# Moving the q, k and attention-gate projections into one stage with the SSD scans

## The reference, cut to what matters

```python
h = rms_norm(x, norm_in);  proj = h @ w_in          # 1024 -> q k v z_attn z_ssd xbc dt_f dt_b
xbc = silu(depthwise_conv(xbc))                     # x (16 heads x 64), B, C (2 groups x 128)
y_ssd = rms_norm((ssd_scan(x, dt_f, B, C) + flip(ssd_scan(flip(...dt_b...))) + d_skip * x) * silu(z_ssd))
#   per chunk of 128 tokens: lmat = exp(acum_l - acum_s) for s <= l;  y_diag = (C B^T * lmat) @ (x * dt)
#   states are carried from chunk to chunk;  y_off = (C @ state) * exp(acum)
y_attn = dilated_mixture(rotary(q), rotary(k), v) * silu(z_attn)   # windows 128/1, 512/4, 2048/16
out = rms_norm(x + concat(y_ssd, y_attn) @ w_out)
```

## Time and profile before

| | us |
|---|---|
| median of 3 runs | 4325.24 (4322.37 to 4328.68) |
| the profiled execution | 4329.58 |
| its span | 4328.0 |
| granted TensorE clock, mean | 0.940 |
| PE busy, DVE busy, ACT busy, POOL busy | 3837.7, 2332.8, 1266.6, 1890.2 |

### The profile page before, as it was taken

How to read it: one execution, slowest core, us unless ns; L and a number is a source line. 1 busy time by engine, 2 the same in 40 slices (tenths; PEclk the granted TensorE clock), 3 DMA queues, 4 the chain that set the end, 5 groups by cost and what they waited for, 6 DMA issues and landing times. The chain is left out here.

```text
span 4328.0 us, 59482 instructions
## 1 busy us (share of the span) xinstructions
PE 3837.7 (89%) x21061; PEld 2920.7 (67%) x21061; DVE 2332.8 (54%) x4451; ACT 1266.6 (29%) x3501; POOL 1890.2 (44%) x1451
## 2 busy tenths in 40 slices
PE   6999999999899998876777777688989999699999
PEld 5887778887788887752333333566666777588887
DVE  4401534403524205416888888577777888556564
ACT  2011220011220012210222222566666777322222
POOL 5444253534344444406999999332233233200000
PEclk9999999999999999988888888899999999799999
DMA  4333242322243232317222222544444344444442
GB/s 160 98 97 94 70 138 88 104 93 79 73 142 102 92 105 65 95 53 288 72 88 89 92 90 76 130 114 107 111 109 116 105 127 118 149 166 152 157 153 108
DMA packets 332015, 483.38 MB, mean 112 GB/s; under 512 B 27772, under 2 KB 228548, under 8 KB 329732
## 3 DMA queue, kind: packets, MB, share of 16 engines
q1 hardware_dynamic: 300867, 365.58, 26.5%
q0 software_dynamic: 26304, 94.78, 7.5%
q10 hardware_dynamic: 4608, 19.92, 1.4%
HBM read 315.04 MB, written 165.15 MB: 111 GB/s over the span
## 5 line engine op out<-in xcount | busy, mean ns | idle before, releaser
L253 POOL TENSOR_TENSOR front_w_hi<-front_w_raw,one 128x1024 fp32r<-128x1024 f32 (+1 forms) x168 | 303.0, 1803 | 929.9 <-PE front_out L475 918.4
L1488 ACT ACTIVATE attn_p_sb<-attn_p_sb,attn_o_sb 128x256 f32<-128x256 f32 (+1 forms) x1152 | 534.9, 466 | 305.1 <-DVE attn_o_sb L1522 300.7
L1522 DVE CUSTOM_DVE_ANT_0 attn_p_sb<-attn_s_ps,attn_mask 128x256 f32<-128x256 f32 (+1 forms) x1152 | 368.7, 376 | 166.1 <-DMA s_o<-attn_o_sb 125.9
L406 DVE TENSOR_SCALAR front_acc<-front_chan,front_consts 128x1024 f32<-128x1024 f32 (+2 forms) x36 | 38.9, 1080 | 714.3 <-ACT front_chan L296 714.3
L1315 POOL COPY attn_q_apart<-attn_q 128x128 f32<-128x128 f32 (+2 forms) x256 | 136.7, 534 | 645.5 <-PE attn_s_ps L1421 639.6
L256 POOL TENSOR_TENSOR front_w_lo<-front_w_raw,front_w_hi 128x1024 fp32r<-128x1024 f32 (+1 forms) x168 | 411.4, 2449 | 13.2
L475 PE MATMUL front_out<-front_h_hi,front_w_hi 128*128 128x512 f32 x1392 | 358.6, 401 | 8.9 <-DVE front_turned L386 3.6
L475 PE MATMUL front_out<-front_h_hi,front_w_lo 128*128 128x512 f32 x1392 | 346.3, 391 | 0.0
L475 PE MATMUL front_out<-front_h_lo,front_w_hi 128*128 128x512 f32 x1392 | 344.0, 389 | 0.0
L960 PE MATMUL ssd_seg<-ssd_spread,masks 128*128 128x512 f32 x384 | 250.3, 793 | 95.4 <-POOL ssd_spread L899 95.4
L475 PE MATMUL front_out<-front_w_hi,front_h_hi 128*128 128x512 f32 x1152 | 291.2, 394 | 29.0 <-POOL front_w_lo L256 29.0
(11 more groups left out here) (178 smaller groups left out, 6882.1 us busy)
## 6 DMA issues: line engine op xcount, KB each, us to landing
front_w_raw<-w_in POOLq DMA_DIRECT2D x156, 512.0 KB, 4.3
s_o<-attn_o_sb SPq DMA_DIRECT2D x288, 132.0 KB, 2.1
output_parts<-s_o SPq DMA_DIRECT2D x24, 1584.0 KB, 6.6
back_xb<-s_xb ACTq DMA_DIRECT2D x24, 640.0 KB, 6.2
ssd_xb<-s_xb SPq DMA_DIRECT2D x24, 640.0 KB, 4.0
s_q<-front_stage SPq DMA_DIRECT2D x48, 256.0 KB, 2.2
s_k<-front_stage SPq DMA_DIRECT2D x48, 256.0 KB, 2.2
s_zs<-front_stage SPq DMA_DIRECT2D x48, 256.0 KB, 3.5
```

The source lines that it names most:

```text
L253: nc.gpsimd.tensor_tensor(hi, raw, one.to_broadcast([P, 2, cols]), ALU.mult).then_inc(sem["w_hi_ready"], 1)
L406: nc.vector.tensor_scalar(a, chan[:, 0:conv.tokens], consts[:, conv.ct:conv.ct + 1], consts[:, TAPS * CHAN_TILES + conv.ct:TAPS * CHAN_TIL ...
L1488: last = nc.scalar.activation(cut, cut, ACT.Exp, scale=-1.0, bias=o_sb[g // 2 % ring][:, g % 2, h, VW:OW], accum_out=o_sb[g // 2 % ring][: ...
L1522: last = nc.vector.tensor_tensor_reduce(out=p_sb[g % 4][:, h, 0:width], in0=s_ps[g % 2][h][:, 0:width], in1=mask[:, step.pattern.strip(ste ...
```

## The change

q, k and za leave front (six of its fourteen groups; 144 units in all). Before the next block's `h` overwrites them, SP stores `h_hi` and `h_lo` of the first two blocks in DRAM (`scratch["h"]`); the third block's stay in SBUF. The backward-states and SSD stages are gone as stages of their own. After stats (which gets two more results: ln dt and the sums, laid out in `wide`) a short stage, `decay_rows_phase`, turns the 48 tiles of `wide` in six rounds (PE eight transposes, ACT a 128x1024 copy, DVE a 128x1024 operation) and stores 1.57 MB and twice 0.39 MB.

Then `late_phase` runs 144 **slots**. In each slot every engine does first a piece of the scans and then its share of one projection unit (24 matmuls, as in front). Slots 0 to 23 hold one backward chunk each; slots 24 to 143 hold 24 forward chunks of five parts each (`CYCLE`). Blocks are taken in the order 2, 1, 0, with q, k, za in each (48 units); at the change of a block ACT loads h half by half (4.19 MB a half). Weights come in pieces of 128 columns, 72 of them, split by POOL. Units of q and k are rotated by DVE, those of za get a Silu on ACT. za is now stored by channel, not by token, so the output stage reads it with 512-byte rows and applies it after the turn.

The scan itself is computed otherwise. The segment sums come from two fp32r matmuls with 64 rows of contraction and 512 columns (`decays`) on rows from DRAM, for forward and backward decay in a bank each; ACT copies the one, DVE overlays the other where s > l by `copy_predicated` (`choose`), ACT takes one exponential over 128x2048, and DVE multiplies by C·B from PSUM (`whole_m`, two of 128x1024). POOL's spreading and the 128x2048 additions on DVE are gone. POOL has, per chunk, `scale_x`, `keep_state`, `skip_x` and the two additions of `add_rest`, 128x1024 each. DVE has four `choose`, two `state_part` (128x1024, PSUM), two `next_state` (128x512, PSUM), two halves of `whole_m`, `gated` (two of 128x1024, one of them from PSUM), `finish`, and four small ones in `skip_part`. PE has four `decays`, `products`, two `state_part`, two `add_state` and `diagonal`, all but `decays` as before.

The core of the diff:

```diff
-    groups = [("rope", "q", 0), ("rope", "q", 1), ("rope", "k", 0), ("rope", "k", 1), ("silu", "zs", 0),
-              ("silu", "zs", 1), ("silu", "za", 0), ("silu", "za", 1), ("chan", "xbc", 0), ("chan", "xbc", 1),
+    groups = [("silu", "zs", 0), ("silu", "zs", 1), ("chan", "xbc", 0), ("chan", "xbc", 1),
               ("chan", "xbc", 2), ("dt", "dt", 0), ("v", "v", 0), ("v", "v", 1)]
...
                 j = t % BT
+                if t >= BT:
+                    act.wait_ge(sem["h_stored"], 32 * (t // BT))
                 nc.scalar.copy(h_hi[:, :, j * P:(j + 1) * P], tr[:, :, :]).then_inc(sem["h_high"], 1)
...
+                if unit.name == "zs" and unit.part == 1 and unit.j == 0 and unit.b + 1 < BLOCKS:
+                    sp.wait_ge(sem["h_split"], (unit.b + 1) * BT)
+                    for i, h in enumerate((h_hi, h_lo)):
+                        sp.dma_start(scratch["h"][unit.b, i, :, :, :], h[:, :, :].bitcast(F32)).then_inc(sem["h_stored"], 16)
...
+    units, ropes = [], 0
+    for turn, b in enumerate((2, 1, 0)):
+        for name in ("q", "k", "za"):
+            for pair in range(D_ATTN // (2 * P)):
+                for half in range(BLOCK // CW):
+                    for ab in range(2):
+                        unit = LateUnit(len(units), turn, b, name, pair, half, ab)
...
+            nc.gpsimd.memset(m[:, :, :], 0.0).then_inc(sem["f_rows_set"], 1)
+            for step, first in enumerate((0, HEADS, 64, 64 + HEADS)):
+                pool.wait_ge(sem["f_rows_set"], step + 1)
+                nc.gpsimd.affine_select(out=m[:, :, :], in_=m[:, :, :], compare_op=ALU.not_equal, fill=1.0,
+                                        base=-first, pattern=[[-1, HEADS], [0, P]], channel_multiplier=1
+                                        ).then_inc(sem["f_rows_set"], 1)
...
+            def split(w):
+                if w >= weights:
+                    return
+                if w >= 3:
+                    pool.wait_ge(sem["l_out"], last_use[w - 3] + 1)
...
+            weigh(0)
+            for slot in range(len(units)):
+                if slot + 1 < first_forward:
+                    weigh(slot + 1)
+                n, part = part_of(slot)
+                if part == 0:
+                    scale_x(n)
+                    keep_state(n)
+                if slot % 4 == 0:
+                    split(slot // 2 + 2)
+                if part == 2:
+                    skip_x(n)
+                if slot % 4 == 3:
+                    split(slot // 4 * 2 + 3)
+                if part == 4:
+                    add_rest(n)
...
+            for slot, unit in enumerate(units):
+                if slot < first_forward:
+                    store_back(slot)
...
+                n, part = part_of(slot)
+                if part == 1 and n:
+                    store_y(n - 1)
+                    load_gate(n)
+                if part == 4 and n + 1 < NT:
+                    load_rows(n + 1)
+                    load_states(n + 1)
+                if part == 1 and 2 <= n + 1 < NT:
+                    load_x(n + 1)
...
+                if slot:
+                    store(units[slot - 1])
...
+            def multiply(unit):
+                u, s = unit.u, unit.weight % 3
+                if unit.n >= 2:
+                    name, count = units[unit.n - 2].taken_by
+                    pe.wait_ge(sem[name][u], count)
+                if unit.turn and unit.n == first_of_half[unit.turn, unit.half]:
+                    pe.wait_ge(sem["l_h_in"][unit.half], 32 * unit.turn)
...
+            def scan(slot):
+                if slot < first_forward:
+                    add_back(slot)
+                n, part = part_of(slot)
+                if part == 0:
+                    if n:
+                        diagonal(n - 1)
+                    decays(n, 0)
+                elif part == 1:
+                    decays(n, 1)
+                    products(n)
+                    state_part(n, 0)
+                elif part == 2:
+                    decays(n, 2)
+                    add_state(n, 0)
+                elif part == 3:
+                    decays(n, 3)
+                    add_state(n, 1)
+                    state_part(n, 1)
+            for slot, unit in enumerate(units):
+                scan(slot)
+                multiply(unit)
+            diagonal(NT - 1)
...
+            def load_h(turn, half):
+                act.wait_ge(sem["l_out"], last_of_half[turn - 1, half] + 1)
+                b = (2, 1, 0)[turn]
+                cut = slice(half * CW, (half + 1) * CW)
+                for i, h in enumerate((h_hi, h_lo)):
+                    act.dma_start(h[:, :, cut].bitcast(F32), scratch["h"][b, i, :, :, cut]).then_inc(sem["l_h_in"][half], 16)
...
+            def rotate(unit):
+                u = unit.u
+                dve.wait_ge(sem["l_out"], unit.n + 1)
+                if u == 0:
+                    if unit.ropes_before:
+                        dve.wait_ge(sem["l_staged"][1], units[unit.n - 1].n // 2 if not units[unit.n - 1].rope else unit.n // 2)
+                    for a in range(2):
+                        last = nc.vector.tensor_tensor(a_turned[:, a, :], out[0][:, :], table[:, a, half], ALU.mult)
+                    last.then_inc(sem["l_taken"][0], 1)
+                    return
+                for a in range(2):
+                    dve.wait_ge(sem["l_stored"][a], 16 * (unit.n // 2))
+                    last = nc.vector.tensor_tensor(stage[:, a, :], out[1][:, :], table[:, 1 - a, half], ALU.mult)
+                last.then_inc(sem["l_taken"][1], 1)
+                dve.wait_ge(sem["l_taken"][1], unit.ropes_before // 2 + 1)
+                for a, op in ((0, ALU.subtract), (1, ALU.add)):
+                    nc.vector.tensor_tensor(stage[:, a, :], a_turned[:, a, :], stage[:, a, :], op
+                                            ).then_inc(sem["l_staged"][a], 1)
...
+            def gated(n):
+                dve.wait_ge(sem["f_rest"], 2 * n + 2)
+                dve.wait_ge(sem["f_diag"], n + 1)
+                nc.vector.tensor_tensor(y[:, :], y[:, :], work[:, :], ALU.add).then_inc(sem["f_y_steps"], 1)
+                dve.wait_ge(sem["f_y_steps"], 2 * n + 1)
+                dve.wait_ge(sem["f_gate_in"], 16 * (n + 1))
+                nc.vector.tensor_tensor(gate[:, :], y[:, :], gate[:, :], ALU.mult).then_inc(sem["f_y_steps"], 1)
...
+            def scan(slot):
+                if slot < first_forward:
+                    back_step(slot)
+                n, part = part_of(slot)
+                if part == 0:
+                    if n:
+                        gated(n - 1)
...
+                    choose(n, 0)
+                elif part == 1:
+                    choose(n, 1)
+                    if n:
+                        finish(n - 1)
+                    skip_part(n)
+                    state_part(n, 0)
+                elif part == 2:
+                    choose(n, 2)
+                    next_state(n, 0)
+                elif part == 3:
+                    choose(n, 3)
+                    next_state(n, 1)
+                    state_part(n, 1)
+                elif part == 4:
+                    whole_m(n)
...
+            for slot, unit in enumerate(units):
+                scan(slot)
+                if unit.rope:
+                    if unit.turn < 2 and unit.n == first_of_half[unit.turn, 0]:
+                        dve.wait_ge(sem["l_rope_in"], 16 * (unit.turn + 1))
+                    rotate(unit)
...
+            def gated(n):
+                dve.wait_ge(sem["e_gate_in"], 16 * n + 16)
+                dve.wait_ge(sem["e_turned"], 2 * n + 2 + 2)
+                flat = gate[:, :, :].rearrange("p k l -> p (k l)")
+                nc.vector.tensor_tensor(flat, tr[1][:, :], flat, ALU.mult).then_inc(sem["e_gated"], 1)
```

975 lines of the change are left out of this document (519 added, 456 removed).

## The result

The changed kernel takes 4060.19 us (median of 4 runs, 4051.55 to 4063.36), beside 4324.0 for the kernel before in the same series. The ratio is 0.9385, with a 95% interval from 0.9373 to 0.9396. So 264 us are gained where I had forecast 337. The range held the time, the sign was right, and the sum was 72 us too optimistic. The profiled execution has a span of 4059.7 us. In the rows PE is TensorE, DVE is VectorE, ACT is ScalarE, POOL is GpSimd and SP is SyncE.

What follows compares the result with a forecast made beforehand. PE was taken to bound front, POOL and DVE the scan stages. Late stage 1191.4 us plus 7 + 22 + 12 gives 1232.4 added, less 1569.9 removed: -337.5, so 3992 profiled, 3988 us forecast; range 3905 to 4115.

Steps and rivals of the forecast that it cites:

- statistics and decay rows: After front: 7 us more in stats, and 22 us (bounds 15 and 35) for the new decay rows stage.
- late: start: Start of the late stage: 33 us of idle PE behind POOL's clear, four selections and first weights (20 to 45).
- The loads of h: Block changes in the late stage: loads hide at 420 GB/s, not at 207; 3 us a change, 6 us charged.
- rival 3: h traffic at 207 GB/s: stores and loads stall PE 72 instead of 18 us, 58 more in all: 4046; chance 0.08.
- The stores of h: Front's zs1 groups, first two blocks: results queue behind each store (D = 25 us), PE stalls 2 x 6 = 12 us.
- The waits in order of lists: Late stage, in-order engine queues: 1.5 us a forward chunk and 0.5 us a backward slot, 48 us.
- rival 2: DVE and POOL set the pace in crowded late-stage parts by contention on two-SBUF operations (+38, +84): 4110; chance 0.17.
- The clock: Late stage: PE busy over 90% at a clock near 1.00; forecast wrong if it falls under 0.9.
- The port: DVE operations on two SBUF tiles can wait for a whole POOL operation, 2.4 us.
- PE's own work: Late stage: PE needs 38.3 us a forward chunk of five slots and 7.15 us a backward slot, no overlap taken.
- Rivals 1: Everything hides: no late-stage waits, free h traffic, short start, half-array pairs side by side: 3887; chance 0.13.
- rival 4: Late-stage slots don't overlap, PE waiting for DVE's work of the slot before: 684 us more, 4624; chance 0.05.

Runs made afterwards that it cites:

- e3: Changed kernel without the stores and loads of h and their waits (values wrong for blocks 0 and 1): ratio 0.9273, 49 us saved.
- e5: Changed kernel with h stored in 16 pieces of 0.52 MB, one ahead of each of 16 units: ratio 0.9338, 20 us saved.
- e1: Changed kernel with VectorE doing whole_m before the rotation of the fourth slot's tile in the forward part: ratio 0.9255, 56 us saved.
- e4: Changed kernel with GpSimd's scan products and sums on one head of 16 (values wrong), weight splits kept: ratio 0.9248, 59 us saved.
- e12: Changed kernel with M first, backward state step first, h stores in pieces, reordered start, split h waits, and backward projection stores one slot later: ratio 0.9163.

## Why the prediction was right, and what it missed

The core was right: front was bound by PE, the scan stages were not, and the same 144 units beside the scan cost their own time and a little more. Point by point, in the spans of the two traces:

| term | forecast, us | found, us |
|---|---|---|
| front, with the stalls of its h stores | -771.4 | -762.7 |
| statistics and decay rows | +29 | +24.8 |
| scan stages removed | -786.5 | -786.3 |
| late: start | 33 | 29.6 |
| late: 24 backward slots, with waits | 183.6 | 194.8 |
| late: forward part without waits and h | 919.8 | 933.8 |
| late: waits in forward | 36 | 53.4 |
| late: loads of h | 6 | 31.7 |
| late: tail | 13 | 11.5 |
| attention and output | 0 | +1.1 |

- **The loads of h were sized wrongly, 26 us.** This is the line of the table that is furthest off. I let them take 10 us at 420 GB/s or 20 at 207 and took 3 us a change. The rate was fine (370 to 400 GB/s), but 4.19 MB do not move alone: weights, x, gate, states and a table share the engines, and the first half landed after some 24 us. The price is that of rival 3 (30 us for the loads), not for its reason of a low rate. Run e3 puts all h traffic at 49 us, where the sum had 18 and rival 3 had 72.
- **The stores of h were placed rightly.** Two pauses of 6.5 and 6.7 us in the zs1 groups (6 forecast), with the low halves landing after 24.4 and 24.5 us (25 assumed). A store of a result issued behind the first of them, at 102.1, landed after 21.5 us, where such stores take 2.0 in the median. What the sum lacks is the half clock behind each pause: 18.6 us come back in e5, not 12. Front is 2 us further off, and why stays open.
- **The waits in order of lists: right in kind, wrong in place and price.** I charged 48 us and put them on the chain from `add_rest` to `choose`. That chain costs little (5.6 us of waiting). The real ones are M behind a rotation (8 times) and the backward state behind a rotation (5 times), both because operations with two SBUF tiles run long beside GpSimd. Together 75 us, between my sum and rival 2, whose mechanism (contention on operations with two SBUF tiles) this is, at other places than it named. Runs e1 and e4 show it from both sides.
- **The clock.** I had the late stage at a clock near 1.00. It was 0.95 to 0.96, and no term of the sum had a price for a wait beyond its own length. That is missing in each of the three points above: in the late stage 60 us of waiting cost 107.
- **The port.** I bounded the delay of one operation by a whole GpSimd operation, 2.4 us. One operation was held up by 3.4 us, behind two of GpSimd's. The contention itself appeared on operations with two SBUF inputs and not on L1262 or L1245, which read PSUM. The Trainium skill's "GPSIMD Engine Reference", section "Specifications", has contention with VectorE instructions that have two SBUF inputs; the trace agrees.
- **PE's own work** was 14 us dearer than 38.3 us a chunk (38.91). In an undisturbed chunk, from start to start, the five units take 28.9 us and not 27.2, and the scan's products 10.0 and not 11.1. The two lean on each other: an f32 group ahead of a unit takes 1.32 us instead of 1.71, and the unit's first eight products 2.24 instead of 1.81 (from 1704.95 to 1707.19). What the 0.6 us a chunk left over come from stays open. The two products with 64 rows take 0.42 to 0.44 us from start to start, so they do not run side by side, as assumed. Backward slots agree (7.21 against 7.15).
- **Smaller terms:** `copy_predicated` takes 0.74 us (0.69 forecast). The four selections take 2.0 us each (2.15 from start to start), not 2.8; the line through the two rows that I named gives 1.9, so my 2.8 was a slip, and the start of 33 us was nearly met for other reasons. Statistics and rows were 4 us shorter than forecast. VectorE is busy 52% of the forward part, under my 60 to 75%. Output and attention did not move, as forecast: the gate's load, now in rows of 512 bytes and queued behind 512 KB instead of 1584 KB, lands after 4.8 us in the median (7.3 before).

Rivals 1 and 4 did not happen. That the time lies well inside the range owes something to luck: no bound of it had the half clock in it, and the room came from rivals 2 and 3. For rival 4 (slots that don't overlap, 2.3 us of waiting in each) the trace has 18 of 23 backward slots without any wait.

## What to carry to other kernels

When work of a stage that is short of one engine is laid beside work that is short of others, add up the busy times first, but then price each wait of the bounding engine above its length if the trace shows its clock falling behind such waits. Here all 60 us of waiting cost 107, and the 18 us of short waits that e1 removed gave back 48 to 56. Walk each in-order list, SyncE's too, and ask for every item whose result is due soonest: one line moved up in VectorE's list was worth 56 us of 4067, and one store moved back in SyncE's turned a reordering that lost 9 us into one that gained 15. Large stores should be cut into pieces among the stage's small ones, as e5 shows; for the loads of h this was not tried. A large load has to be asked for by the rate that is left beside the others, not by the rate of an empty queue.

## What the runs showed of the hardware

- Idle spells of TensorE of only 2.1 to 3.6 us in full-clock work were mostly followed by work at 1.2 GHz: ten of 13 in the late stage of the changed kernel, in the stretch shown above for some 7 us (from the clock column, (1 - 0.73)/0.5 x 4.9 + (1 - 0.51)/0.5 x 4.3). Three of 2.14, 2.55 and 2.51 us were not; behind the first of these the next chunk lost 0.1 us (42.65 us, then 38.99). Spells of the same length went both ways, so length alone does not decide at these lengths.
- A VectorE operation with two SBUF inputs (1.21 us alone) was recorded at 4.63 us beside GpSimd, ending behind two whole GpSimd operations although its record begins before them; in e12 one like it was recorded at 6.72 us, beside two products and a selection of GpSimd. Those that read PSUM stayed within 2 ns (1220 to 1222 ns for L1262).
- From 1612 us on, around a change of block, the DMA engines of the core moved 356 to 400 GB/s, at a busy share above 1.0 as the profile counts it; transfers of h_lo (2.1 and 4.2 MB) took 22.9 to 25.6 us, where pieces of 0.5 MB spread over front took 3.6 and 4.3 us in the median.
